# Layer 0 begun on half of the channels, and attention whose outputs are scaled by turned reciprocals in a reordered loop of steps

## What is computed

```
mod = (silu_c @ w_mod[l] + b_mod[l])              # six sections of 1024: shift, scale, gate, twice
h   = rmsnorm(x, g_attn[l]) * (1 + sc_a) + sh_a   # needs sections 0 (shift) and 1 (scale)
u   = h @ w_in[l]                                 # 5632 columns
...
s = concat([s_win, s_ctx, sink_col]) ; p = softmax(s)
o = p[window] @ v + p[context] @ vc               # 6 + 6 heads, 64 wide
```

## Time and profile before

| | us |
|---|---|
| median of 3 runs (1333.46 to 1334.05) | 1333.49 |
| the profiled execution, own time | 1334.14 |
| its span in the trace | 1332.3 |
| start of layer 0's projection | 39.0 |
| layer 0's attention on PE, from the scores of step 2 to the last A | 160.2 to 242.9 |
| the same in layer 1 | 881.2 to 931.1 |

### The profile page before, as it was taken

One profiled execution on the slowest core, in us unless ns is written; L12 is line 12 of the kernel. 1 busy time (PEld: TensorE's weight loads), 2 busy tenths in 40 slices (PEclk: granted clock), 3 DMA queues, 4 the chain that ended last, 5 costly groups with the idle time before them and its releaser, 6 DMA issues.

```text
span 1332.3 us, 22176 instructions
## 1 busy us (share of the span) xinstructions
PE 1213.0 (91%) x8966; PEld 927.0 (70%) x8966; DVE 645.4 (48%) x1503; ACT 440.1 (33%) x1049; POOL 167.0 (13%) x208
## 2 busy tenths in 40 slices
PE   4899987999999999999999889999998878889986
PEld 2787854788888967666666459875998865555652
DVE  1544786464355463422221285587767645324334
ACT  3533366533334351010000265356666610000001
POOL 1810000110010210000000321000111100000001
PEclk9899999999999999999999999999999889999998
DMA  9995145423323269999999995338564989999995
GB/s 352 316 353 177 64 138 188 150 95 95 95 95 127 90 265 416 399 415 413 416 384 373 402 237 149 120 133 278 177 189 145 357 333 413 417 416 413 380 374 192
DMA packets 131831, 351.15 MB, mean 264 GB/s; under 512 B 23053, under 2 KB 84725, under 8 KB 108560
## 3 DMA queue, kind: packets, MB, share of 16 engines
q1 hardware_dynamic: 118144, 317.69, 64.4%
q0 software_dynamic: 12304, 30.37, 6.7%
q10 hardware_dynamic: 1280, 1.66, 0.4%
HBM read 330.53 MB, written 28.86 MB: 270 GB/s over the span
## 4 chain that ended last, share of the span: by engine, by line
PE 81%; DVE 10%; issue 4%; DMA 4%; ACT 2%; POOL 0%; SPq 0%; DVEq 0%; ACTq 0%; POOLq 0%
PE banks L1028 34%; PE banks L1286 16%; PE banks L1300 8%; PE banks L1278 6%; PE banks L1209 4%; PE banks L962 2%; PE banks L1134 2%; PE banks L1149 2%; PE banks L1119 1%; DMA expert_rows<-arena,rows_u 1%; DMA ring<-in_w_in 1%; DMA ring<-in_w_mod 1%; DVE w_lo_r L2042 1%; DVE arena L2461 1%; DVE att L2128 1%
## 5 line engine op out<-in xcount | busy, mean ns | idle before, releaser
L2042 DVE TENSOR_TENSOR w_lo_r<-ring,w_hi_r 128x256 fp32r<-128x256 f32 x480 | 223.0, 475 | 229.5 <-ACT w_hi_r L1641 228.3
L1641 ACT ACTIVATE w_hi_r<-ring 128x256 fp32r<-128x256 f32 x480 | 197.5, 416 | 302.5 <-PE banks L1028 255.3
L1286 PE MATMUL banks<-ring,arena 128*64 128x256 f32 x2016 | 232.5, 383 | 21.5 <-DVE arena L2429 8.6
L1028 PE MATMUL banks<-h_hi_r,w_hi_r 128*128 128x512 f32 (+1 forms) x640 | 221.9, 347 | 5.7 <-DVE h_lo_r L1988 5.6
L1028 PE MATMUL banks<-h_lo_r,w_hi_r 128*128 128x512 f32 (+1 forms) x640 | 220.2, 344 | 0.0
L1028 PE MATMUL banks<-h_hi_r,w_lo_r 128*128 128x512 f32 (+1 forms) x640 | 220.0, 344 | 0.0
L1286 PEld LDWEIGHTS banks<-ring,arena 128*64 128x64 f32 x2016 | 161.9, 138 | 81.7 <-issue 31.2
L1028 PEld LDWEIGHTS banks<-h_hi_r,w_hi_r 128*128 128x128 f32 x640 | 122.3, 191 | 22.2 <-ACT arena L1611 5.0
L1300 PE MATMUL banks<-ring,att 128*64 128x512 f32 x424 | 119.7, 609 | 15.2 <-issue 7.8
L1028 PEld LDWEIGHTS banks<-h_lo_r,w_hi_r 128*128 128x128 f32 x640 | 122.5, 191 | 13.9
L1028 PEld LDWEIGHTS banks<-h_hi_r,w_lo_r 128*128 128x128 f32 x640 | 122.4, 191 | 13.9
(11 more groups left out here) (274 smaller groups left out, 1704.3 us busy)
## 6 DMA issues: line engine op xcount, KB each, us to landing
ring<-in_w_e_gate SPq DMA_DIRECT2D x64, 1024.0 KB, 8.9
ring<-in_w_e_up SPq DMA_DIRECT2D x62, 1024.0 KB, 9.3
ring<-in_w_e_down SPq DMA_DIRECT2D x53, 1024.0 KB, 9.3
ring<-in_w_mod SPq DMA_DIRECT2D x48, 1024.0 KB, 6.5
ring<-in_w_in SPq DMA_DIRECT2D x38, 1024.0 KB, 5.6
expert_rows<-att POOLq DMA_DIRECT2D x23, 512.0 KB, 20.3
ring<-in_w_o SPq DMA_DIRECT2D x8, 1024.0 KB, 5.1
ring<-in_w_branch SPq DMA_DIRECT2D x8, 640.0 KB, 4.6
```

The source lines that it names most:

```text
L1028: ins = mm(out_ap, a, b, start=k == 0 and p_ == 0, stop=k == KD - 1 and p_ == 2)
L1286: ins = mm(banks[e * CAP:(e + 1) * CAP, bank, 0:DE], x[:, k, e * CAP:(e + 1) * CAP], w[:, k * DE:(k + 1) * DE], start=k == 0, stop=k == KD ...
L1641: fn(w_hi[:, u % AHEAD, :, :], chunk(key)[:, q * KU:(q + 1) * KU, :], ACT.Copy).then_inc(w_hi_ready, 1)
L2042: v.tensor_tensor(w_lo[:, u % AHEAD, :, :], chunk(key)[:, q * KU:(q + 1) * KU, :], w_hi[:, u % AHEAD, :, :].bitcast(F32), ALU.subtract).th ...
```

## The change

Three parts, in one kernel.

**Channels.** Channel groups are contiguous now (128k to 128k+127), so the rows of `w_in` are loaded as `(k p)` instead of `(p k)`. Sections 1 and 0 of layer 0 are loaded, multiplied, biased and turned in two halves of 512 channels each (`mod_half`, `half_columns`). The first half of both is 4 MB through the ring; the second half, 4 MB too, goes to other buffers behind the first two chunks of `w_in`. The first three chunks of `w_in` (HALVED) are taken in halves: units 0 to 3 of each, then units 4 to 7 of each. `lift` moves the transposed tokens of groups 4 to 7 out of PSUM, ahead of the splits. Turning a section takes 8 matmuls of 128x128 weights and 2 columns where it was 32 of 128x32 weights; layer 1's two sections (at the end of layer 0's experts) are turned that way as well.

**Scaling.** The probabilities are no longer scaled. DVE widens the reciprocals to 128x2x64, PE transposes them (two instructions for a pair of steps, behind A, in the same bank), ACT copies A's result out as before (`o_raw`), and DVE multiplies it with the turned reciprocals (called Mul below, `o_ready`).

**Order.** PE makes Sc1 directly behind Sc0, ahead of A and T. ACT does Ev first in a turn. DVE does Red before Rec, and `mod_add` and Mul last.

```diff
+                if l == 0:
+                    for half in range(2):
+                        for n, key in enumerate(HALVED):
+                            mine = [(o, arg[0]) for o, (what, ch, arg) in enumerate(OUTS[0]) if what == "chan" and ch == key[2]]
+                            split_units(key, [(banks[:, OUT_BANK[o], :], side) for o, side in mine], chan_sides((NTOK, NTOK)),
+                                        proj_done, (h_lo_ready, 0) if n == 0 else None,
+                                        units=range(UNITS // 2 * half, UNITS // 2 * (half + 1)))
+                            if half == 0 and n == 1:
+                                for sec in (1, 0):
+                                    for j in range(2):
+                                        mod_half(sec, 1, j)
+                                half_columns(1)
+                    pe.wait_ge(col_ready, 4)
...
                     if s % 2:
                         if 0 < s and s + 2 < n:
                             scores(l, s + 1, 0)
+                            scores(l, s + 1, 1)
...
-                    if s % 2 and 0 < s and s + 2 < n:
-                        scores(l, s + 1, 1)
...
+                pe.wait_ge(recip_ready, g + 2)
+                for b in range(2):
+                    ins = turn(banks[:, O_BANK, (2 + b) * P:(3 + b) * P],
+                               recip[:, g // 2 % 2, b, :, :].rearrange("p e m -> p (e m)"), ident)
                 ins.then_inc(pv_done, 1)
```

DVE, `begin` of layer 0 and the end of a turn of `attention`:

```diff
+                    lift(4)
+                    lift(6)
                     for q in range(AHEAD):
                         split_w(key, q)
+                    for half in range(2):
+                        dve.wait_ge(col_ready, 2 * (half + 1))
+                        k0 = 4 * half
+                        full(k0)
+                        for k in range(k0 + 1, k0 + 4):
+                            full(k)
+                            rest_h(k - 1)
+                        rest_h(k0 + 3)
+                        for halved in HALVED[1 - half:3 - half]:
+                            for q in range(k0, k0 + 4):
+                                split_w(halved, q)
+                        if half == 0:
+                            mod_add_half(1)
+                            half_columns(1)
...
-                        link(v.reciprocal(rsum[:, b, :], esum[:, b, :]))
-                        for q in range(2):
-                            ins = v.tensor_scalar(S[b][:, q, 0:k], S[b][:, q, 0:k], rsum[:, b, q:q + 1], None, ALU.mult)
-                        ins.then_inc(p_ready, 1)
...
+                        link(v.reciprocal(r, esum[:, (s - 1) % 3, :]))
+                        v.tensor_copy(recip[:, (g - 1) // 2 % 2, :, (s - 1) % 2, :], r.unsqueeze(2).to_broadcast([P, 2, HD]))\
+                            .then_inc(recip_ready, 1)
...
+                    if s % 2 == 0 and 0 <= s - 4 < n:
...
+                        dve.wait_ge(o_raw, (g - 4) // 2 + 1)
+                        v.tensor_tensor(o, o, banks[:, O_BANK, 2 * P:4 * P], ALU.mult).then_inc(o_ready, 1)
```

## The result

The changed kernel took 1326.63 us (median of 6 runs, 1324.89 to 1329.91) where the kernel before took 1334.26 beside it: ratio 0.993, interval 0.9909 to 0.9951. It was measured three more times: 0.9964 (0.9941 to 0.9986), 0.9944 (0.9922 to 0.9965) and 0.9914 (0.9897 to 0.993). Each ratio is taken against the kernel before, run beside it. So the change is faster by 0.4 to 0.9%, some 7 us. The forecast was 1332.1 us, with a range of 1328.5 to 1335.5: the first measurement lies outside it.

A forecast was written before the change was run, and what follows sets the result against it. PE, busy 91% of the span, was taken to bound the kernel. Start −1.2, layer 0's attention −1.35, layer 1's +0.7 and columns +0.5 sum to −1.35 from 1334.14; median forecast 1332.1 us, range 1328.5 to 1335.5.

The forecast's parts named there:

- the attention's sum: Both layers' attention: 82.75 us to fall by 1.35 in layer 0, 49.9 to rise by 0.7 in layer 1.
- latent loop: Attention's latent pairs: DVE's queue from PTc to STT sets the cycle, 8.74 us against 8.05 before.
- allowance: Attention: 0.1 us added per pair, eight in layer 0, five in layer 1, because the old kernel's cycle came out 7.9 for 8.05.
- Where PE stood: Whole kernel: PE is busy 91% of the span, so time saved at the changed places passes through.
- The start, −1.2: Start to projection: projection begins at 30.85, 8.15 us earlier, 6.95 given back later; net −1.2 us, bounds −3 and +1.
- Rival B: Latent pairs: DVE's loop doesn't bind, pairs go at PE's 8.16 and 8.3 us; total 1329.0 us, chance 0.20.
- The walk: Attention added up cycle by cycle: 80.6 us in layer 0 against 82.75, 50.1 in layer 1 against 49.9.
- Context pairs: Attention's context pairs: Sc1 covers the copy's wait, so A no longer idles; 5.16 us against 5.57.
- Columns, +0.5: Layer 1's section columns: 32 wide records against 2.15 us before, half hidden by waits for experts' weights; +0.5 us, bounds −1 and +2.
- Rival C: Projection's first stretch: clock stays low after PE's pauses, some 40 matmuls slower; +7.5 us, 1339.6 us, chance 0.09.
- D: Start gives nothing, its 8.15 us taken back whole, and layer 1's columns lie fully on the path; 1333.8 us, chance 0.19.

The follow-up runs named there:

- att_only: Kernel before plus only the attention hunks (turned reciprocals, Mul, new order), old start; ratio 0.9965, second set 0.9934.
- start_only: Changed kernel with the attention hunks undone, keeping the new start and wide columns; ratio 1.0001, second set 0.9988.
- mul_late: Changed kernel with Mul moved behind the next step's STT; layer 0's attention 78.44 us, layer 1's 48.31; ratio in a second set 0.9915.
- narrow_all: Changed kernel with columns turned in the narrow 128x32 form at the start and for layer 1; layer 1's columns took 3.6 us.
- after_third: Changed kernel unchanged, a third set of times and a third profile; ratio to before 0.9944.
- after_4: Changed kernel unchanged, measured and profiled a fourth time; ratio to before 0.9914.
- after: The changed kernel itself, here its first profile; median 1326.63 us, ratio to the kernel before 0.993, profiled execution 1329.73 us.
- after_again: Changed kernel unchanged, run for a second profile and more times; ratio to before 0.9964.
- scaled_new_order: Changed kernel with the new order kept but probabilities scaled as before; attention 105.59 us in layer 0, 57.82 in layer 1.

## Why the prediction was wrong

The step that failed is the attention's sum. It put −1.35 and +0.7 us where the traces show −3.31 and −0.62, by a latent loop worked out too long (8.74 for 8.41) and an allowance added for nothing. Behind that stands a part of the measured saving that no term of the prediction and no stretch of the traces holds. Term by term:

**Where PE stood.** Right: the places. That a saving passes through is seen for attention, whose 3.9 us come back in the time of both sets of `att_only` (4.7 and 8.8 us).

**The start, −1.2.** Near: −1.07 in the first profile, with the projection at 30.98 for 30.85 and, of the 39.00 − 30.98 = 8.02 gained, 8.02 − 1.07 = 6.95 given back, as worked out. Some of this is luck. The first piece was ready at 14.60 and not at 13.72, and the walk behind it took 16.4 us instead of the 17.1 worked out; the two errors cancel. In the other traces of the changed kernel the walk took 16.7 to 17.2 and the gain came out between −2 and +0.7 us, in `start_only` near nothing.

**The latent loop.** The mechanism was right and its size off: "Sum **8.74**" was 8.41. Scores of both key sets took 1.93 (174.03 to 175.96) and not 2 × 1.06, and Mul followed the widening after 0.14, the price of a copy from 181.17 to 181.31, not 0.25. The lower bound that I had given for it (0.13) was near the true one. T to PTc was 1.12, Red 1.13, Mul 0.33. Taken by themselves, the widening has a mean of 0.227 us (36 of them) and Mul 0.416 (18); the estimates from the page's cycles (the Trainium skill, VectorE: DVE Perf Modes, The TRN2 errata) were 0.19 and 0.39, both a little short, and the loop goes by starts anyway. (By these two the six cycles give back 0.24 us and not about 0.3.) Three cycles in each layer make 1.0 us in each. Rival B fell, though its 1329.0 lies nearer to the measurement than the forecast: the scores did wait for L2295, and `mul_late` shows by how much.

**The allowance.** This step failed outright: "so I add 0.1 for each of eight pairs", and as much for five pairs in layer 1. The walk gave 80.6 and 50.1. Less the 1.0 in each layer that is 79.6 and 49.1, and the traces show 79.44 and 49.26 without any allowance. The gap that the walk had on the kernel before (7.9 for 8.05) doesn't show in the new loop, and there was no reason to carry it over. So attention gave −3.31 and −0.62 where I wrote −1.35 and +0.7, an error of 3.3 us, the largest single one: 2.0 of it is the loop, 1.3 the allowance. Context pairs were right (5.13 for 5.16).

**Columns, +0.5.** The whole 1.48 (3.63 for 2.15) came at PE's step; the half that I took off for waiting experts has no ground in the trace. Nor is it the wide form's price, as the narrow form of `narrow_all` shows the same there (3.6).

**What no term had.** The phases sum to −1.1 − 3.3 − 0.6 + 1.5 = −3.5, which from the profiled 1334.14 gives a median of 1334.14 − 3.5 − 0.65 = 1330.0. That is inside the stated range. What carries the measured 1326.63 out of it is the rest: the profiled executions differ by 4.4 (1334.14 and 1329.73), the four measurements by 5 to 11. Over all runs 1.3 us of the difference go with the clock, and 2.9 us at equal clock are left over. They can't be put down to one part: attention gives 5.2 where its stretches save 3.9, the start 0.9 where its phases lose 0.4, and in the first set `att_only` gained only 0.8 us beyond its stretches. No stretch of the traces shows it for certain. From layer 1's attention to the end the changed kernel and `att_only` take 398.7 to 400.6 us and the kernels with the old attention 400.0 to 403.9, but `mul_late` 402.4 and 402.5, in a stretch where the clock dips now here, now there. It stays open.

**Rival C.** It was seen, in small. In `after_third`, and in the same way in `mul_late`, the clock was low again after the second pause; in `after_4` it fell six matmuls later, at 50.1. That is three of the eleven traces with the new start and wide columns. Timeline of `after_third`, and its window from 50 to 60 us and that of `after_4`, with the columns of the earlier trace rows:

```profile
48.43 2.22 PE L1034 MATMUL banks<-consts,modr 128*128 128x2 f32 x16 [0.61 <-DVE modr L2078]
50.51 0.77 PE L1106 MATMUL banks<-h_hi_r,w_hi_r 128*128 128x512 f32 x1
51.08 0.63 PE L1106 MATMUL banks<-h_lo_r,w_hi_r 128*128 128x512 f32 x1
```

```profile
50.00:60.00 10.00, 10.00 (x40) 8.26 (x40) 6.26 (x15) 6.14 (x13) 10.00 (x16) 0.83 0.93 152
50.00:60.00 10.00, 10.00 (x39) 8.08 (x38) 5.79 (x13) 5.62 (x13) 9.71 (x16) 0.83 1.04 166
```

Seven matmuls of `after_third` start 0.3 to 0.57 us apart there instead of 0.23, on top of fourteen slow ones at the start where after has nine: PE reached the scores of step 2 at 160.21 from a projection at 30.13, 130.08 us, where after took 128.05. In `after_4` it took 128.68. The price is up to 2 us when it comes, far from the 7.5 of the rival. What it would have taken to stay at the higher level wasn't tried. D fell as a whole, since attention saved more, but its core held in `start_only`: the start gives nothing by itself.

## What to carry to other kernels

Price a new loop by start-to-start times of neighbouring rows, walk it once, and add nothing for an unexplained rest of the old loop. Before making a small operation smaller, take it out of the queue ahead of the one that PE waits for: Mul cost 0.33 us per pair there and nothing one place later. An order of steps and a set of waits belong together: here each half of the attention change alone was slower in layer 0 (by 0.8 and 23 us), and together they saved 3.3. And a saving of 2 or 3 us in 1330 needs the traces to be seen: the times of one pair of kernels gave 5 to 11 us in four measurements.

## What the runs showed of the hardware

In `scaled_new_order` five T of layer 0 waited 2.90 to 2.96 us. Behind four of them PE worked at the lower level, 1.81 to 1.97 us for eight transposes that take 1.06; behind the fifth (200.30) the clock stayed at 1.00 and they took 1.09. A pause from one projection matmul to the next of some 6 us, filled with 128 small matmuls and 16 column matmuls (128x2), was followed by the lower clock in three traces and by the higher in eight, with the same program on both sides (`after_third` and `after_4` against after and `after_again`).

Matmuls with two columns didn't cost the same from place to place. 128 narrow ones took 2.2 us in the kernel before and 3.5 to 4.2 in four traces of other kernels at the same place; in `narrow_all` 116 of them ran at 10 ns each and PE then stood 2.15 us without a releaser. In the start 16 wide ones took 1.81 and 64 narrow ones 1.94.
